# A diffusion trunk on one core: the short convolution's in-projection, block by block or as Strassen pairs of panels

## What is computed

```python
def _short_conv_mixer(h, w_in, w_conv, w_out, rows):
    gate_b, gate_c, xin = jnp.split(h @ w_in, 3, axis=-1)      # h (1024, 1024), w_in (1024, 3072)
    u = gate_c * xin
    y = _dwconv(u.reshape(b * rows, GRID_W, d), w_conv).reshape(b, l, d)   # three taps along rows of 64
    return (gate_b * y) @ w_out
```

## Time and profile before

| what | value |
|---|---|
| median of three runs | 2596.21 us |
| the profiled execution, its own time | 2599.73 us |
| its span, first to last instruction | 2597.7 us |
| mean granted clock of TensorE | 0.991 of full speed |
| busy: PE, DVE, ACT, POOL | 97%, 67%, 43%, 48% of the span |
| chain that ended last: share of PE | 84% |
| first FFN's pairs in the loop | about 1000 to 1310 us |
| convolution's blocks 1 to 7 | 1609 to 1844 us |

### The profile page before, as it was taken

One profiled execution on the slowest core, in us unless ns is written; L12 is line 12 of the kernel. 1 busy time (PEld: TensorE's weight loads), 2 busy tenths in 40 slices (PEclk: granted clock), 3 DMA queues, 4 the chain that ended last, 5 costly groups with the idle time before them and its releaser, 6 DMA issues.

```text
span 2597.7 us, 35777 instructions
## 1 busy us (share of the span) xinstructions
PE 2526.1 (97%) x12452; PEld 2115.8 (81%) x12452; DVE 1745.5 (67%) x2334; ACT 1112.6 (43%) x2089; POOL 1242.3 (48%) x810
## 2 busy tenths in 40 slices
PE   7999999999999999999999999999999999999998
PEld 5888888888878778888888877888787888888886
DVE  5377777767865466667667986666436555566898
ACT  5334534443443553343445475111264433434444
POOL 3121321432230047776768961444304776766983
PEclk9999999999999999999999999999999999999999
DMA  6223432441361443343456332323514223345533
GB/s 261 72 72 126 179 134 70 154 146 60 119 257 67 138 142 130 122 145 129 166 204 237 98 110 100 123 103 111 219 49 154 106 92 106 118 167 213 194 99 114
DMA packets 119634, 351.04 MB, mean 135 GB/s; under 512 B 12241, under 2 KB 12241, under 8 KB 116433
## 3 DMA queue, kind: packets, MB, share of 16 engines
q1 hardware_dynamic: 119504, 349.33, 38.5%
HBM read 258.58 MB, written 90.70 MB: 134 GB/s over the span
## 4 chain that ended last, share of the span: by engine, by line
PE 84%; DVE 7%; POOL 2%; ACT 2%; issue 2%; DMA 2%; SPq 1%; DVEq 0%; ACTq 0%; POOLq 0%
PE psum L1420 19%; PE psum L1422 19%; PE psum L1421 19%; PE psum L2005 4%; PE psum L2007 4%; PE psum L2006 4%; PE psum L1680 2%; PE psum L1682 2%; PE psum L1681 2%; PE psum L1632 2%; POOL row_unit_sum L1377 1%; PE psum L1619 1%; PE psum L1646 1%; PE psum L1454 1%; PE psum L1602 1%
## 5 line engine op out<-in xcount | busy, mean ns | idle before, releaser
L1420 PE MATMUL psum<-x_hi,unit 128*128 128x512 f32 x1232 | 481.3, 391 | 6.7 <-DVE x_lo L2746 6.7
L1421 PE MATMUL psum<-x_lo,unit 128*128 128x512 f32 x1232 | 480.0, 390 | 0.0
L1422 PE MATMUL psum<-x_hi,unit 128*128 128x512 f32 x1232 | 479.8, 389 | 0.0
L2746 DVE TENSOR_TENSOR c_set<-c_set,psum 128x512 f32<-128x512 f32 x352 | 233.8, 685 | 275.4 <-ACT c_set L2102 178.7
L1328 POOL TENSOR_TENSOR unit<-unit_sum,unit 128x512 fp32r<-128x512 f32 x200 | 293.8, 1477 | 5.8 <-ACT unit L2102 4.8
L1420 PEld LDWEIGHTS psum<-x_hi,unit 128*128 128x128 f32 x1232 | 231.9, 188 | 55.9 <-issue 4.1
L1422 PEld LDWEIGHTS psum<-x_hi,unit 128*128 128x128 f32 x1232 | 231.7, 188 | 48.2
L1421 PEld LDWEIGHTS psum<-x_lo,unit 128*128 128x128 f32 x1232 | 231.8, 188 | 47.7
L1420 PE MATMUL psum<-h_hi,w_hi 128*128 128x512 f32 x624 | 262.6, 421 | 1.8 <-DVE h_lo L2746 1.8
L1422 PE MATMUL psum<-h_hi,w_lo 128*128 128x512 f32 x624 | 244.2, 391 | 0.0
L2005 PE MATMUL psum<-row_unit_hi,part_hi 128*128 128x512 f32 x616 | 241.2, 392 | 3.0 <-DVE part_lo L2746 1.8
(11 more groups left out here) (321 smaller groups left out, 5636.8 us busy)
## 6 DMA issues: line engine op xcount, KB each, us to landing
ffn_raw<-in_w_ffn_in SPq DMA_DIRECT2D x80, 512.0 KB, 5.2
part_raw<-parts_kept SPq DMA_DIRECT2D x154, 256.0 KB, 2.7
parts_kept<-part_sums SPq DMA_DIRECT2D x22, 1280.0 KB, 5.3
out_raw<-in_w_ffn_out SPq DMA_DIRECT2D x44, 512.0 KB, 7.7
w_raw<-in_w_hgrn_in SPq DMA_DIRECT2D x40, 512.0 KB, 3.6
ada_raw<-in_ada SPq DMA_DIRECT2D x32, 512.0 KB, 4.9
conv_ada_raw<-in_ada SPq DMA_DIRECT2D x32, 512.0 KB, 4.3
units_kept<-stage_unit SPq DMA_DIRECT2D x28, 512.0 KB, 2.9
```

The source lines that it names most:

```text
L1420: begin = pe.matmul(out_ap, hi[:, a:b], rhs_hi, start=first, stop=False)
L1421: pe.matmul(out_ap, hi[:, a:b], rhs_lo, start=False, stop=False)
L1422: return begin, pe.matmul(out_ap, lo[:, a:b], rhs_hi, start=False, stop=last)
L2746: V.tensor_tensor(dst, a, b, op).then_inc(S[sem], 1)
```

## The change

Of the eight blocks, two (0 and 1) stay as they are. The 18 panels of blocks 2 to 7 are taken as nine pairs (for two blocks: C and x of the first, C and x of the second, B of both), each by the seven products of the FFN's scheme. For this DVE makes nine sums of quarters of the activations, each 128 x 2048, and ACT and DVE split five of them (`conv_parts`). Blocks 0 and 1 still need their taps and gates at the same time. After a C-and-x pair DVE multiplies the two results, ACT writes the centre tap as a scaled copy (`conv_centre`), and DVE adds the side taps in the next pair (`conv3(..., centre=False)`). The last split of the result (`conv_low`) moves to the end. POOL splits of panels in blocks 2 to 7 go; `total` and `low` of the pairs come, and the low parts of three out-projection rows (`row_low`) after pairs 2, 3 and 8.

The modulation groups are shared out anew: eight instead of four in the first FFN's loop (two panels a pair in place of one, `ada_sums` every two pairs), and four instead of eight in the convolution (over pairs 0 to 7). All loads of the convolution's modulation work now go by the half-panel buffers, which follow DVE's use.

```diff
-G_CONV = G_FFN + 4
+G_CONV = G_FFN + 8
+CONV_GROUPS = 4
+PLAIN_BLOCKS = 2
+CONV_PAIRS = 3 * (KB - PLAIN_BLOCKS) // 2
 ...
+def conv_panels(p):
+    blk, which = PLAIN_BLOCKS + p // 3 * 2, p % 3
+    return ((3 * blk, 3 * blk + 1), (3 * blk + 3, 3 * blk + 4), (3 * blk + 2, 3 * blk + 5))[which]
 ...
 # SyncE, first FFN's loop
                         pair_loads(i * 4 + (4 + e), e)
                         if f == 0:
-                            ada_halves(i * ADA_GROUP + (ADA_GROUP * G_FFN + e))
+                            for k in range(2):
+                                ada_halves(i * (2 * ADA_GROUP) + (ADA_GROUP * G_FFN + 2 * e + k))
 ...
 # SyncE, convolution
+            for p in range(2):
+                conv_pair_loads(p)
+                conv_ada(p)
+            sp.wait_ge(S["gemm_full"], O_END)
+            sp.wait_ge(S["x_summed"], len(X_SUMS[0]) + CONV_SUMS)
+            for r in range(2):
+                conv_row_load(r)
+            for p in range(2, CONV_PAIRS):
+                conv_pair_loads(p)
+                if p < 2 * CONV_GROUPS:
+                    conv_ada(p)
 ...
 # GpSimd, convolution
+                for p in range(CONV_PAIRS):
+                    for l in range(PRODUCTS):
+                        if l + 1 < PRODUCTS and l + 1 in SUMMED:
+                            total(p, l + 1)
+                        elif l + 1 == PRODUCTS and p + 1 < CONV_PAIRS:
+                            ready(p + 1)
+                            total(p + 1, 0)
+                        if l in SUMMED:
+                            low(p, l)
+                    if p in (2, 3):
+                        row_low(p - 2)
+                row_low(2)
 ...
 # TensorE, convolution
             conv_first_panels()
-            ada_sums(G_CONV)
             conv_block(1, 1)
-            with pe.Fori(1, KB // 2) as i:
-                conv_block(i * 2, 0)
-                conv_block(i * 2 + 1, 1)
+            for p in range(CONV_PAIRS):
+                conv_pair(p)
+                if p % 2 == 1:
+                    ada_sums(G_CONV + p // 2)
 ...
 # VectorE, first FFN's pair
                     if ada_of is not None:
-                        ada_rows(ada_of, e, 1)
+                        ada_rows(ada_of, e % 2 * 2, 1)
                     for a, l in ((1, 1), (2, 2), (3, 3), (4, 3), (5, 4), (6, 4)):
                         add_to(a, l)
+                    if ada_of is not None:
+                        ada_rows(ada_of, e % 2 * 2 + 1, 1)
 ...
 # VectorE, convolution
+            conv_sum(conv_t21, *conv_quarter(0, 1), ALU.add)
+            conv_sum(conv_t22, *conv_quarter(1, 1), ALU.add)
+            conv_sum(conv_parts[M7][2], conv_t21[:, :, :], conv_t22[:, :, :], ALU.add, SUM_T22)
+            conv_block(0, 6)
+            conv_gate(0)
+            conv_sum(conv_t11, *conv_quarter(0, 0), ALU.add)
+            conv_sum(conv_parts[M4][2], conv_t21[:, :, :], conv_t11[:, :, :], ALU.subtract, SUM_T11)
+            conv_sum(conv_parts[M1][2], conv_t11[:, :, :], conv_t22[:, :, :], ALU.add)
+            conv_sum(conv_t12, *conv_quarter(1, 0), ALU.add)
+            conv_sum(conv_parts[M3][2], conv_t12[:, :, :], conv_t22[:, :, :], ALU.subtract, SUM_T12)
+            conv_sum(conv_t12, conv_t11[:, :, :], conv_t12[:, :, :], ALU.add)
+            conv_part_low(M4)
+            conv_block(1, 4)
+            conv_unit_low(0, M4)
+            conv_part_low(M3)
+            conv_unit_low(0, M3)
+            conv_part_low(M1)
+            conv_gate(1)
+            conv_part_low(M7)
+            for p in range(CONV_PAIRS):
+                conv_pair(p)
+            for blk in range(KB - 2, KB):
+                conv_low(blk, 0)
+            for blk in range(KB):
+                conv_low(blk, 1)
```

More of the change, by code:

```diff
@@ L273, in row_loads @@
 def row_loads(r, stage):
-    return 16 * sum(r in rows for rows in (range(KB), range(FFN_GROUPS - 4), range(SPLIT_CONV, KB),
+    return 16 * sum(r in rows for rows in (range(KB), range(FFN_GROUPS - 4), range(KB),
                                            range(FFN_GROUPS - 4))[:stage + 1])
@@ L528, in build_trunk @@
     conv_u = at("conv_u", 160, [P, SEQ])
-    conv_v = at("conv_v", 164, [P, SEQ])
     conv_c = at("conv_c", 188, [P, SEQ])
@@ L1232, in split @@
                 split_to(n, slot, places[slot], late)
-            def splits(n0, n1, places, late=0):
-                with pool.Fori(n0 // 2, n1 // 2) as i:
-                    for slot in range(2):
-                        split(i * 2 + slot, slot, places, late)
             def panel_low(n, slot, place):
@@ new lines, in conv_gate, with conv_sum, conv_quarter @@
+            def conv_gate(blk):
+                dve.wait_ge(S["gemm_evac"], blk * 6 + (4 + O_CONV + 6))
+                dve.wait_ge(S["conv_done"], blk * 5 + 9)
+                tt(conv_m[blk][:, :], conv_m[blk][:, :], conv_b[:, :], ALU.mult, "conv_done")
+            def conv_sum(dst, one, other, op, after=0):
+                if after:
+                    dve.wait_ge(S["x_summed"], len(X_SUMS[0]) + after)
+                tt(dst[:, :, :], one, other, op, "x_summed")
+            def conv_quarter(half, second):
+                return tuple(as_f32(conv_h[part][half][:, 4 * second:4 * second + 4, :]) for part in range(2))
@@ new lines, in conv_part_low, with conv_unit_low @@
+            def conv_part_low(kind):
+                hi, lo, total = (part[:, :, :] for part in conv_parts[kind])
+                dve.wait_ge(S["x_hi"], len(X_PARTS[0]) + CONV_HIGH_ORDER.index(kind) + 1)
+                tt(lo, total, hi, ALU.subtract, "x_ready")
+            def conv_unit_low(p, l):
+                unit = conv_unit(p, l)
+                dve.wait_ge(S["unit_hi"], PRODUCTS * (PAIRS + p) + l + 1)
+                tt(unit[1][:, :], conv_terms(p, l)[0], unit[0][:, :], ALU.subtract, "unit_low")
@@ new lines, in conv_pair @@
+            def conv_pair(p):
+                last, blk, c0 = p == CONV_PAIRS - 1, PLAIN_BLOCKS + p // 3 * 2, conv_done_after(p - 1)
+                group = G_CONV + p // 2 if p < 2 * CONV_GROUPS else None
+                if group is not None:
+                    ada_rows(group, p % 2 * 2, 1)
+                if p > 0 and (p - 1) % 3 < 2:
+                    first = conv_sets[(p - 1) % 2][:, 0:2, :].rearrange("p a n -> p (a n)")
+                    conv3(PLAIN_BLOCKS + (p - 1) // 3 * 2 + (p - 1) % 3, first, conv_done_after(p - 2), centre=False)
+                for a in range(1, 7):
+                    conv_add(p, a)
+                    if last and a in (4, 6):
+                        for b in range(3):
+                            conv_low(3 * (a // 6) + b, 0)
+                    if p == 0 and a == 1:
+                        conv_part_low(M6)
+                if group is not None:
+                    ada_rows(group, p % 2 * 2 + 1, 1)
+                conv_add(p, 7)
+                if not last:
+                    conv_unit_low(p + 1, M4)
+                    conv_unit_low(p + 1, M3)
+                conv_add(p, 8)
+                if group is not None and p % 2 == 1:
+                    ada_bias_add(group)
+                first, second = (conv_sets[p % 2][:, 2 * i:2 * i + 2, :].rearrange("p a n -> p (a n)") for i in range(2))
+                dve.wait_ge(S["c_added"], added_after(0, PAIRS + p, PAIR_ADDS))
+                if p % 3 < 2:
+                    tt(first, first, second, ALU.mult, "conv_done")
+                else:
+                    dve.wait_ge(S["conv_done"], c0)
+                    for i, gate in enumerate((first, second)):
+                        tt(conv_m[blk + i][:, :], conv_m[blk + i][:, :], gate, ALU.mult, "conv_done")
```

395 lines of the change are left out of this document (281 added, 114 removed).

## The result

The changed kernel takes 2631.14 us (median of four, 2629.65 to 2632.47), the kernel before 2596.03 (2593.95 to 2596.23): a ratio of 1.0137 (95% interval 1.0119 to 1.0154), 35 us slower. The forecast was 2606 with a range up to 2622: the side was right, the size outside the range. The profiled execution of the changed kernel has a span of 2628.3 us, 30.6 more than before, at a mean clock of 0.984.

A forecast was written before the change was run, and what follows sets the result against it. PE, busy 97% of the span, was taken as the bound. Terms -24.5 - 0.4 + 15.3 + 1.5 + 4 + 13.6 = +9.5 us gave 2606 us against the runs' median, range 2578 to 2622.

The forecast's parts named there:

- Matmuls, -24.5: Convolution: 864 matmuls become 756, 108 less at 0.227 us each, -24.5 us.
- 0.4: Convolution block 1: a short PE stall for a POOL split with a late-loaded panel goes, -0.4 us.
- Hand-over, +15.3: From block 1 to pair 0: PE waits for late DVE and POOL work, +15.3 us, bounds 0 and 20.
- the clock, +1.5: Hand-over: half a stretch at the lower clock after the last wait, +1.5 us (0 to 5).
- M3's 1.4: Hand-over, pair 0: product M3 waits 1.4 us for a split of 2.2 and its unit.
- Steady pairs, +4: Convolution pairs: taps cost 1.2 us and `row_low` after pairs 2 and 3 costs 2.8, +4 us (0 to 9).
- The 1.2 us for taps: Steady convolution pairs: a pair with taps just passes; 0.2 us for each of six, 1.2 us.
- The first FFN's loop, +13.6: SP's queue delays raw panels, so PE waits 1.7 us in each of eight even pairs; bounds 0 and 22.
- A: Faster rival: POOL and DVE don't hold each other up in the new places; 2581 us, chance 0.25.
- B: Rival: late panels in the FFN's loop are harmless, all else as forecast; 2592 us, chance 0.22.
- C: Slower rival: the FFN loop's eight waits bring the clock down, 1.5 to 2 us more each; 2620 us, chance 0.10.
- my row of 385: FFN's loop: the trace's 385 GB/s while stores and panels move, used instead of the skill's 358.

The follow-up runs named there:

- the end of the series: Against the best kernel before it, the last pair's second modulation row on DVE moved ahead of the result's three splits: 2585.23 us, ratio 0.9953.

## Why the prediction was wrong, step by step

- *Matmuls, -24.5:* right. 108 fewer; where PE waits for nothing a pair takes 19.04 us (M2 of pairs 1 and 2 start at 1673.84 and 1692.88 in the run with two sums early), forecast 19.0; at the end of the series, with the waits mostly out, the convolution takes 271.4 us against 294.6 before, and 24.5 + 0.4 + 3.2 for the moved sums would make 266.5.
- *Hand-over, +15.3, and the clock, +1.5:* right. The waits at M4, M1, M7 and M6 are 2.52, 0.47, 2.80 and 4.79 us, and 0.66 in the next pair, 11.2 in all, with 16 slow matmuls at 0.2 us, 3.2: 14.4, where the two terms have 16.8. M6 came 61.3 us after `conv_u` of block 0 started, forecast 63.6. M3's 1.4 did not come. One reason was incomplete: I put M6 down to the queue's order, and with that mended the wait only moved. The backlog of DVE, 53 us of work and holds without a gap, is the cause: reordering left it where it was, and taking two sums out of it paid back about what they were worth.
- *Steady pairs, +4:* the row parts cost 1.79 and 1.57 us (forecast 1.4 each), with 7 slow matmuls behind the second, 1.4. The 1.2 us for taps did not show as waits. Together 4.8. With these terms the convolution would be 8.9 us shorter than before; it is 6.7 shorter, so some 2 us of it are found in no term.
- *The first FFN's loop, +13.6:* **this step failed.** The mechanism was right, SP's queue held the odd pair's panels back; its size was not, and the clock behind the waits stood in it at nothing. With the sums set aside the step cost 39.9 - 3.2 = 36.7 us. Three sizes make the difference of 23. First, the panels were there 16.0 us into the even pair, my upper bound, not 14.9: the modulation row that frees the half ends at 5.2 us and the stores are issued at 5.95, since DVE comes to this row only 3.0 us into the pair and its second instruction takes 1.67 us, where the earlier trace rows has 0.75 as the median and 1.69 as the longest. That makes waits of 3.0 us on average, 23.7 in all, 10 above the forecast. The bound on a wait, 2.8 us, was exceeded in five of the eight. Secondly the clock: 9 us. Thirdly delays of 0.1 to 0.3 us at many units, about 4 us by difference.
- *Rivals:* A and B fell, with the hand-over and with the late panels. C, the clock falling behind the eight waits, had a chance of 0.10 and came true in six of eight. It was priced on top of waits of 1.7 us, so its 2620 was low too: with 3.0 us waits it gives about 2630. The evidence that I set against it, the 1.9 us idle from 1963 on the earlier trace rows, was of a shorter wait, and its window ends 0.65 us behind that wait; 3.21 us with a clock of 0.50 behind it stood in the same group, and waits near my own upper bound of 2.8 were nearer to that. The trace of the kernel before also had, just ahead of that window, a wait of 2.03 us with the lower clock behind it, which my argument left out:

```profile
1954.51 0.66 PE L1453 MATMUL psum<-ident,x_scaled 128*128 128x128 f32 x4 [2.03 <-ACT x_scaled L2102]
...
1956.00:1959.00 3.00, 3.00 (x10) 2.52 (x9) 0.15 (x1) 2.98 (x9) 2.86 (x4) 0.50 0.29 119
```

The two terms hang together: whoever takes the bound for the one must take the other. I added them as if one could come without the other.

The range failed for the same reason. The high ends of the sum give 2627 (-24.9 + 20 + 5 + 9 + 22, on 2596), not the 2625 that I wrote, without the clock in the loop, and I cut the range at 2622. Of the 35 us in the medians the spans account for 30.6; the rest is the difference between the profiled executions and their medians.

The two rules of the Trainium skill. DVE's long sums hold POOL and are held by it, as SBUF — State Buffer, Who interferes with whom, says: the 8.29 us for two sums and the 3.35 us `total` agree. DMA: Bandwidth & Descriptors, Specifications, gives about 358 GB/s, by which the panels would be half a microsecond later than from my row of 385. The window at 1137 shows 343 GB/s, one from 1134 to 1142 has 361 and one from 1135 to 1137 has 406, above the page's figure; the panels came 10.0 us after the first store, where I had 9.9 with the added half-panel. The mean rate is nearer the page's figure, the time nearer mine.

## What to carry to other kernels

When work is added to a loop, price the place of its loads in the queue before the work itself: here the second modulation panel itself cost PE 6.6 us at most, and its wait ahead of the weight panels cost 29 us. Give a wait near 3 us its stretch at half clock from the start, in every pair in which it comes. And before reordering a hand-over, find the engine with the backlog and an idle time ahead of it: orders that hand the backlog on gave nothing in four runs, moving two sums into 8 us of idle time gave 4 us in the medians and 6 in the profiled convolution.

## What I had not expected of the hardware

How loosely the clock's price hangs on the length of a wait. In the FFN's loop alone it looks like a matter of length: fourteen waits of 0.4 to 1.1 us cost no clock, one of 2.07 us was followed by 8 matmuls at 1.2 GHz, and of eight waits of 2.7 to 3.2 us six were. But one wait of 2.72 us has a stretch behind it and another of 2.72 has none, nor has the longest, 3.23. In the convolution of the changed kernel the wait of 1.79 us behind the first row part has none and the one of 1.57 us behind the second has. At that same place the kernel with the FFN's panels ahead waits only 1.12 us, and the clock is at 0.50 there too:

```profile
1743.87 0.47 PE L1545 MATMUL psum<-conv_h_hi,conv_unit_hi 128*128 128x512 f32 x1 [1.12 <-POOL conv_unit_lo L1512]
...
1745.00:1747.00 2.00, 2.00 (x6) 1.52 (x6) 2.00 (x2) 0.00 (x0) 0.70 (x1) 0.50 0.00 0
```

What else decides, these runs don't tell.
